# A three-block network on one core: the fifth feed-forward network by seven products, and an earlier or later place for the token sums of the others

## The reference

```python
def _swiglu(h, w_in, w_out):
    a, b = jnp.split(h @ w_in, 2, axis=-1)
    return (jax.nn.silu(a) * b) @ w_out

for layer in range(2):
    x = x + 0.5 * _swiglu(_rmsnorm(x, ffn_norm[layer, 0]), ffn_w_in[layer, 0], ffn_w_out[layer, 0])
    x = x + mixer(_rmsnorm(x, mix_norm[layer]))
    x = x + 0.5 * _swiglu(_rmsnorm(x, ffn_norm[layer, 1]), ffn_w_in[layer, 1], ffn_w_out[layer, 1])
```

```python
x = x + g2 * swiglu(modulate(rms_norm(x, norm2_gain), sh2, sc2), w_ffn_in, w_ffn_out)
return rms_norm(x, final_gain)
```

## Time and profile before

| | |
|---|---|
| timed runs | 2793.37 us median of 3 (2790.82 to 2793.62) |
| profiled execution | 2790.73 us, span of its instructions 2789.1 us |
| mean granted TensorE clock | 0.999 |
| instructions | 35799, of them 14740 matmuls |
| HBM read | 284.78 MB, 103 GB/s over the span |
| network 0, input units | 7.49 to 249.03 us (first output unit) |
| network 4, input units | about 2413 to 2658.73 us (first output unit) |

### The profile page before, as it was taken

How to read it: one execution, slowest core, us unless ns; L and a number is a source line. 1 busy time by engine, 2 the same in 40 slices (tenths; PEclk the granted TensorE clock), 3 DMA queues, 4 the chain that set the end, 5 groups by cost and what they waited for, 6 DMA issues and landing times. The chain is left out here.

```text
span 2789.1 us, 35799 instructions
## 1 busy us (share of the span) xinstructions
PE 2762.3 (99%) x14740; PEld 2348.8 (84%) x14740; DVE 1728.4 (62%) x2347; ACT 1118.8 (40%) x1328; POOL 39.3 (1%) x77
## 2 busy tenths in 40 slices
PE   8999999999999999999999999999999999999998
PEld 7998887789988899888887899888898988888888
DVE  7897667468886688865665677636555543633333
ACT  5333237443342433424554533424443532422222
POOL 0000000000000000000000000000000000000000
PEclk9999999999999999999999999999999999999999
DMA  4333342123334333343211232324322122222232
GB/s 162 114 121 133 133 138 68 46 98 121 123 121 142 122 112 129 129 138 115 61 46 62 105 114 99 106 104 145 113 73 67 46 91 91 91 90 103 93 106 76
DMA packets 69091, 289.00 MB, mean 104 GB/s; under 512 B 7680, under 2 KB 30336, under 8 KB 40528
## 3 DMA queue, kind: packets, MB, share of 16 engines
q1 hardware_dynamic: 60480, 257.18, 26.8%
q0 software_dynamic: 8032, 29.37, 3.3%
q10 hardware_dynamic: 432, 0.36, 0.0%
HBM read 284.78 MB, written 2.10 MB: 103 GB/s over the span
## 5 line engine op out<-in xcount | busy, mean ns | idle before, releaser
L2552 PE MATMUL PS<-sb_HH,sb_WH 128*128 128x512 f32 (+1 forms) x2168 | 806.6, 372 | 10.8 <-DVE sb_WL L1425 5.8
L2553 PE MATMUL PS<-sb_HL,sb_WH 128*128 128x512 f32 (+1 forms) x2168 | 800.4, 369 | 0.0
L2554 PE MATMUL PS<-sb_HH,sb_WL 128*128 128x512 f32 (+1 forms) x2168 | 800.3, 369 | 0.0
L593 ACT ACTIVATE sb_WH<-sb_RAW 128x2048 fp32r<-128x2048 f32 x238 | 455.2, 1913 | 850.0 <-PE PS L2554 849.3
L1425 DVE TENSOR_TENSOR sb_WL<-sb_RAW,sb_WH 128x2048 fp32r<-128x2048 f32 x207 | 473.6, 2288 | 487.7 <-ACT sb_WH L593 487.7
L2552 PEld LDWEIGHTS PS<-sb_HH,sb_WH 128*128 128x128 f32 x2168 | 409.0, 189 | 86.3 <-issue 6.9
L2554 PEld LDWEIGHTS PS<-sb_HH,sb_WL 128*128 128x128 f32 x2168 | 408.8, 189 | 69.4
L2553 PEld LDWEIGHTS PS<-sb_HL,sb_WH 128*128 128x128 f32 x2168 | 409.1, 189 | 68.7 <-issue 1.4
L2552 PE MATMUL PS<-glh_GHI,sb_WH 128*128 128x512 f32 x704 | 274.4, 390 | 0.0
L2554 PE MATMUL PS<-glh_GHI,sb_WL 128*128 128x512 f32 x704 | 273.9, 389 | 0.0
L2553 PE MATMUL PS<-glh_GLO,sb_WH 128*128 128x512 f32 x704 | 273.9, 389 | 0.0
(11 more groups left out here) (455 smaller groups left out, 3948.9 us busy)
## 6 DMA issues: line engine op xcount, KB each, us to landing
sb_RAW<-in_weights SPq DMA_DIRECT2D x221, 1024.0 KB, 4.8
ff_ADAW<-in_w_ada POOLq DMA_DIRECT2D x48, 512.0 KB, 3.9
sb_RAW<-in_weights SPq DMA_DIRECT2D x39, 512.0 KB, 5.1
out_t<-sb_XT SPq DMA_DIRECT2D x8, 256.0 KB, 2.4
sb_XT<-in_x SPq DMA_DIRECT2D x3, 512.0 KB, 7.7
sb_RAW<-in_weights SPq DMA_DIRECT2D x4, 256.0 KB, 3.7
b_CT<-in_ctx POOLq DMA_DIRECT2D x1, 1024.0 KB, 6.9
hy_BD<-in_c_gates POOLq DMA_DIRECT2D x1, 512.0 KB, 3.5
```

The source lines that it names most:

```text
L593: act.activation(WH[slot][:, :], RAW[slot][:, :], ACT.Copy).then_inc(*T["w_hi"].up())
L2552: pe.matmul(out, wh, xh, start=start, stop=False)
L2553: pe.matmul(out, wh, xl, start=False, stop=False)
L2554: return pe.matmul(out, wl, xh, start=False, stop=stop)
```

## The change

It edits the functions of ScalarE, VectorE and TensorE; the host side, the loads and GpSimd's program are not touched.
- `SEVEN` gets an entry for network 4 (pairs 2 to 9), and network 0's pairs begin at 3 instead of 2. The counts of the semaphores follow from this table.
- Network 4 is made by `ffn_seven` on all three engines. In its path for a network that is not late, VectorE makes `HG` as `HH` + `HL` (two additions of 128 x 2048), then the token sums, then the low half of unit u0+2.
- In networks 1 to 3 ScalarE makes `HG` ahead of `inverse` and not behind it.
- In network 0 ScalarE makes `HG` in pair 1, between the high halves of units 3 and 4, and rounds the token sums at the end of pair 1. VectorE makes the token sums at the end of pair 1, and their low parts in pair 2, between `raw_sums` and `sums_low`.

```diff
-SEVEN = {0: range(2, 10), 1: range(2, 10), 2: range(2, 10), 3: range(2, 10)}
+SEVEN = {0: range(3, 10), 1: range(2, 10), 2: range(2, 10), 3: range(2, 10), 4: range(2, 10)}
...
@@ ScalarE, ffn_seven @@
+                def tokens_whole():
+
+                    for t in range(KT):
+                        last = act.activation(HG[:, t, :], XT[:, t, :], ACT.Copy, scale=gain_of(name, t))
+                    last.then_inc(*T["q_hi"].up())
+
+                def tokens_high(t0, t1):
+
+                    for t in range(t0, t1):
+                        act.wait_ge(T["q_sum"].sem, q_sums(n, SEVEN[n][0], t - 4)[1])
+                        act.activation(TH[:, t, :, :], TF[:, t, :, :], ACT.Copy).then_inc(*T["q_hi"].up())
...
                 else:
                     split(u0 + 1)
+                if late and not lead:
+                    tokens_whole()
                 if late:
                     inverse(m_)
-                    for t in range(KT):
-                        last = act.activation(HG[:, t, :], XT[:, t, :], ACT.Copy, scale=gain_of(name, t))
-                    last.then_inc(*T["q_hi"].up())
                 if rest:
                     rest()
                 if not lead:
                     split(u0 + 2)
                 silu(0)
-                for t in range(4):
-                    act.wait_ge(T["q_sum"].sem, q_sums(n, SEVEN[n][0], t - 4)[1])
-                    act.activation(TH[:, t, :, :], TF[:, t, :, :], ACT.Copy).then_inc(*T["q_hi"].up())
+                if not lead:
+                    tokens_high(0, 4)
                 for i in range(1, FFN_IN // 2):
                     split(u0 + 2 * i + 1)
+                    if lead and i == 1:
+                        tokens_whole()
                     if i in SEVEN[n]:
                         first_product(i)
...
                     if late:
                         silu(i)
+                    if lead and i == 1:
+                        tokens_high(0, 4)
...
-            ffn(4, lambda kt: MOD[:, 24 + kt, 0:1])
+            ffn_seven(4, lambda kt: MOD[:, 24 + kt, 0:1])
@@ VectorE, ffn_seven @@
-                def token_lows():
-
-                    for t in range(4):
+                def token_lows(t0, t1):
+
+                    for t in range(t0, t1):
...
-                if late:
+                if late and not lead:
                     token_sums()
                 for i in range(1, FFN_IN // 2):
                     gated(i - 1)
                     split(u0 + 2 * i + 1)
-                    if i == 1:
-                        token_lows()
+                    if i == 1 and not lead:
+                        token_lows(0, 4)
...
                     if i in SEVEN[n]:
                         scaled_seven(i)
+                    if i == 2 and lead:
+                        token_lows(0, 4)
                     if i + 1 in SEVEN[n]:
                         sums_low(i + 1)
                     else:
                         split(u0 + 2 * i + 2)
+                    if i == 1 and lead:
+                        token_sums()
                     conditioned(ADA_IN.get(i, (0, 0))[1], 7)
...
-            ffn(4, lambda kt: CSC[:, 2, kt:kt + 1], lambda kt: MOD[:, 24 + kt, 0:1], lambda t: MOD[:, 40 + t, 0:1])
+            ffn_seven(4, lambda kt: CSC[:, 2, kt:kt + 1], lambda kt: MOD[:, 24 + kt, 0:1], lambda t: MOD[:, 40 + t, 0:1])
@@ TensorE @@
-            ffn(4)
+            ffn_seven(4)
```

## The result

The changed kernel takes 2776.72 us (median of five runs, 2776.57 to 2778.41). The kernel before took 2793.19 beside it (five runs, 2790.82 to 2793.62). The ratio is 0.9947 [0.9936, 0.9958]. Forecast were 2778.5 us, a range of 2774.5 to 2784.0, and faster. The profiled execution took 2776.75 us with a span of 2775.1, 14.0 less than the 2789.1 of before, where the sum had said 14.0. The medians moved by 16.5. The prediction did not explain that difference between spans and medians, and half of the experiments are about it.

What follows compares the result with a forecast made beforehand. TensorE, with work in 99% of the span, was taken as the bound: -5.7 - 3.3 - 5.0 = -14.0 us gives 2776.7 from the profiled execution or 2779.4 from the median; forecast 2778.5 us, range 2774.5 to 2784.0.

Steps and rivals of the forecast that it cites:

- -6.2 + 0.5 = -5.7: Network 4: eight pairs in seven products gain 0.78 us each, 6.2 together; a new wait at its start costs 0.5.
- The additions without a row: Network 4's start: two 128x2048 additions on VectorE building HG, priced by the 2.28 us subtraction of the same shape.
- The cover: Network 4's steady pairs: VectorE's 9.8 us chain stays hidden behind TensorE's work, cost 0; without it, lateness costs one for one.
- rival 1: Network 4's pairs give nothing because a feed arrives late, VectorE's share rising to some 14 us; 2784.7 us, chance 0.08.
- -3.3: Starts of networks 1 to 3: HG ahead of the inverse removes three HT waits, 1.1 us each with slow first matmuls.
- -5.6 + 0.6 = -5.0: Network 0: unit 4 ends 5.6 us earlier, less a new 0.6 us wait before unit 7.
- the 6.4 us: Network 0, unit 3: ends 17.3 us after 42.1 where 10.9 are work, so 6.4 us lost to wait and slow clock.
- The sum, -14.0: Whole kernel: network 4's -5.7, networks 1 to 3's -3.3 and network 0's -5.0 us added along TensorE's line.
- 1 to 4: Rivals: network 4 gains nothing, 0.08; network 0 keeps its loss, 0.12; network 4 slower, 2798 us, 0.03; HG edit useless, 0.07.
- Rival 2: Network 0 keeps its loss as the wait moves, or short idles make the clock swing; 2783.5 us, chance 0.12.
- rival 4: Networks 1 to 3: the HG edit does nothing because another input takes over the wait; 2781.8 us, chance 0.07.
- two bases: Starting times for subtracting the sum: profiled execution 2790.73 us, giving 2776.7, and median of timed runs 2793.37, giving 2779.4.

## Why the prediction was right, point by point

- **Network 4, "-6.2 + 0.5 = -5.7".** Measured -5.74, alone -5.69. The pair was priced 0.78 and is 0.79; the start 0.5 and is 0.48, by the experiments on each. The additions without a row, taken at 2.28 by the subtraction of the same shape, are 4.49 for two. The cover held: VectorE goes from 7.07 to 12.74 us a pair ("some 14" in rival 1 was too much: this network has no scaling and no conditioning), and TensorE has no wait in it.
- **Networks 1 to 3, "-3.3".** Measured -3.8 in after and -3.1 alone, 1.13 and 1.14 in the two clean stretches. In the third, the wait on `ADAR` adds 0.3 in after and takes 0.3 in the run alone; without it the three are 3.4. The mechanism is the one told: `HG` runs in the time in which ScalarE waited 2.63 us for the sum of squares.
- **Network 0, "-5.6 + 0.6 = -5.0".** Measured -5.06 alone and -4.54 in after. The wait for the first tokens' low parts ended 0.4 us later in that execution (14.31 against 13.89; 13.78 in the run alone), in a place that no edit touches; counted from its end, network 0 is 4.95 shorter in after and 4.92 in the run alone. Unit 4 ended at 64.3 for a forecast of 63.9, and the new wait before unit 7, first slow matmul included, stood 0.7 over the pitch for a forecast of 0.6. Two things in the step were left open and are now known: of the 6.4 us, 1.65 were the clock; and `HG` was not the obstacle, the token sums and their roundings were.
- **The sum, -14.0.** That it met the spans to the tenth is in part luck: the `ADAR` wait gave 0.3 that nobody forecast, and the start of the kernel took 0.4.
- **Rivals.** 1 to 4 did not happen. Rival 2 feared that a short new wait would bring the clock down; it stayed at 1.00 behind the waits of 0.44 and 0.23 us in every profile that has them. One fall was priced at some 1.8 us and took 1.65 in network 0. The place where the clock falls in some executions only, the wait for the keys, is in no part of the prediction. The upper end of the range, 2784.0, covered rival 2 or rival 4 (2783.5, 2781.8), not both (2786.8).
- **From the sum to the time.** This step was only half right. The prediction saw a spread of 2.8 us and put the forecast between two bases without a cause. The cause is two falls of the clock in different places, and filling one wait leaves the spread of the other: 1.5 us in some executions behind the 2.1 us wait for the keys, and up to 1.6 us in the length of the low clock behind the 4.57 us wait. The change removes the second and cannot touch the first. With the keys' wait filled on both sides the medians differ by 2791.44 - 2776.78 = 14.7. In the profiled execution of before, the low clock behind the restart in network 0 was 2.4 us shorter than in that of before with the keys' wait filled (3.4 against 5.8), and the unit there took 1.1 us less, so the traces say 14.0 and other executions more. That neither of the two profiled executions had the fall behind the keys is luck as well: with one of each kind the spans would differ by 1.5 more or less than 14.0. The 16.5 between the shown medians comes on top of that from which level the middle run fell on: three of five runs of before at 2793, one of five of after at 2778.4. Why the clock falls in one execution and not in the next is not shown.

## What to carry to other kernels

Here a kernel bound by one engine was forecast to a few tenths of a us in each stretch by cutting that engine's line at landmarks and pricing each edit by the nearest row, waits at their length plus the slow restart. When runs of one kernel stand in groups, look for the idle stretch of TensorE where the granted clock differs between executions, before a median is compared with a median; filling that stretch with throw-away matmuls shows whether it is the cause. The better repair is to move what stands before the awaited instruction: that gave the wait back (-2.3 us) and left one group of runs, where filling only left one group.

## What the hardware showed that was not expected

- Behind a wait of 2.10 us the granted clock is at its low level of 1.2 GHz for a part of the next 6 us in some executions (a mean of 0.72 and 0.71 in the windows there) and stays at 1.00 in others; the difference is 1.5 us. With that wait gone, five runs lie within 0.35 us, with waits of 1.7 us (before the kernel's first matmul) and 1.2 us still in the kernel.
- Behind a wait of 4.57 us the low level of 1.2 GHz was there in each of the four profiles that have this wait unfilled, but for 3.3 to 5.8 us, worked out from the granted clock in windows (3.3 in the run with `HG` first, 3.4 in the kernel before, 5.7 in the run with network 4 alone, 5.8 in the kernel before with the keys' wait filled). Each us of it costs half a us: 1.65 for 3.4.
- A 256-column matmul takes 120 ns and a 512-column one 227: 13 and 14 ns over their columns at 2.4 GHz. So a pair in which one unit of two has an eighth of its products taken away, 6.25% by count, gains 3.6% (0.78 of 21.76).
